# RWKV scan: key norms and group norms taken by a power of minus one half on GpSimd instead of a square root on ScalarE and a reciprocal on VectorE

## The reference, cut to what matters

```
kkf = split_heads(k * k_k)                       # 16 heads of 64 channels
kk  = kkf / maximum(sqrt(sum(kkf * kkf, -1)), 1e-12)      # the key norm, one number a token and head
...
mu  = y.mean over a head's 64 channels            # the group norm of the scan's output
var = square(y - mu).mean over the same 64
z   = (y - mu) * rsqrt(var + 64e-5) * lnx_g + lnx_b  + bonus, then times the gate
```

## Time and profile before

| | |
|---|---|
| time, median of 3 runs | 3846.18 us (3844.47 to 3848.1) |
| time of the profiled execution | 3840.48 us |
| its span in the profile | 3837.7 us |
| TensorE busy, share of the span | 92% |
| VectorE, GpSimd, ScalarE busy | 63%, 50%, 25% |
| mean granted TensorE clock | 0.967 of full speed |

### The profile page before, as it was taken

How to read it: one execution, slowest core, us unless ns; L and a number is a source line. 1 busy time by engine, 2 the same in 40 slices (tenths; PEclk the granted TensorE clock), 3 DMA queues, 4 the chain that set the end, 5 groups by cost and what they waited for, 6 DMA issues and landing times.

```text
span 3837.7 us, 74279 instructions
## 1 busy us (share of the span) xinstructions
PE 3525.7 (92%) x31772; PEld 3301.6 (86%) x31772; DVE 2402.6 (63%) x3149; ACT 962.6 (25%) x1950; POOL 1930.2 (50%) x1067
## 2 busy tenths in 40 slices
PE   7999999999789878889999994799999999999998
PEld 3877799999788678878999994799999777899997
DVE  5355688757784467746885768887586556622125
ACT  5333230001243355532300012300012333310010
POOL 1323456665365646626566561366564333466662
PEclk9899999999899899989999997899999999999999
DMA  8200134433145534332343331243332100122221
GB/s 322 64 12 17 41 103 138 137 115 117 69 142 180 152 85 103 83 95 66 113 146 120 124 102 41 78 148 128 115 125 69 36 18 18 56 77 77 73 77 50
DMA packets 226855, 367.66 MB, mean 96 GB/s; under 512 B 104752, under 2 KB 111088, under 8 KB 226416
## 3 DMA queue, kind: packets, MB, share of 16 engines
q1 hardware_dynamic: 171408, 255.08, 21.9%
q10 hardware_dynamic: 55136, 107.98, 8.1%
HBM read 326.47 MB, written 36.54 MB: 95 GB/s over the span
## 4 chain that ended last, share of the span: by engine, by line
PE 76%; DVE 12%; ACT 3%; issue 2%; DMA 2%; SPq 1%; POOL 1%; ACTq 0%; DVEq 0%; POOLq 0%
PE ps L851 58%; PE ps L1105 3%; PE ps L894 2%; PE ps L1118 2%; PE ps L1136 2%; DVE r_t L2544 1%; PE ps L911 1%; DVE x L2340 1%; DVE r_hlo L2528 1%; PE ps L1077 1%; PE ps L1059 1%; DVE ps L2693 1%; DVE x L2349 1%; DVE m_mx L2472 1%; DVE s_T L2692 1%
## 5 line engine op out<-in xcount | busy, mean ns | idle before, releaser
L678 POOL TENSOR_TENSOR w_hi<-w_raw,zrow 128x1024 fp32r<-128x1024 f32 x354 | 694.9, 1963 | 1246.6 <-PE ps L851 898.2
L680 POOL TENSOR_TENSOR w_lo<-w_raw,w_hi 128x1024 fp32r<-128x1024 f32 x354 | 900.6, 2544 | 27.8
L2242 DVE SCALAR_TENSOR_TENSOR f_acc<-f_unit,silu_c,f_acc 128x512 f32<-128x512 f32 x504 | 630.7, 1292 | 7.6
L851 PE MATMUL ps<-f_hhi,w_hi 128*128 128x320 f32 x2688 | 635.3, 318 | 0.0
L851 PE MATMUL ps<-f_hhi,w_lo 128*128 128x320 f32 x2688 | 613.7, 310 | 0.0
L851 PE MATMUL ps<-f_hlo,w_hi 128*128 128x320 f32 x2688 | 611.4, 309 | 0.0
L851 PEld LDWEIGHTS ps<-f_hlo,w_hi 128*128 128x128 f32 x2688 | 449.4, 188 | 0.0
L851 PEld LDWEIGHTS ps<-f_hhi,w_lo 128*128 128x128 f32 x2688 | 449.1, 188 | 0.0
L851 PEld LDWEIGHTS ps<-f_hhi,w_hi 128*128 128x128 f32 x2688 | 441.1, 189 | 0.0
L851 PE MATMUL ps<-f_ahi,w_hi 128*128 128x320 f32 x1408 | 322.7, 310 | 0.0
L851 PE MATMUL ps<-f_ahi,w_lo 128*128 128x320 f32 x1408 | 321.1, 309 | 0.0
(11 more groups left out here) (400 smaller groups left out, 6710.4 us busy)
## 6 DMA issues: line engine op xcount, KB each, us to landing
w_raw<-in_w SPq DMA_DIRECT2D x340, 512.0 KB, 3.6
f_unit<-in_ada_w ACTq DMA_DIRECT2D x72, 1024.0 KB, 6.2
ada_ring<-in_ada_w SPq DMA_DIRECT2D x24, 1024.0 KB, 6.5
up_scratch<-r_o ACTq DMA_DIRECT2D x40, 320.0 KB, 2.9
s_LW<-up_scratch SPq DMA_DIRECT2D x16, 320.0 KB, 4.9
s_LA<-up_scratch SPq DMA_DIRECT2D x8, 640.0 KB, 6.7
x<-in_x SPq DMA_DIRECT2D x1, 2560.0 KB, 9.6
x_scratch<-r_o ACTq DMA_DIRECT2D x8, 320.0 KB, 2.2
```

The lines of the kernel that those rows point to most:

```text
L678: nc.gpsimd.tensor_tensor(whi[:, slot, :], raw[:, raw_slot, :], zrow[:, 0:1].to_broadcast([P, CH * P]), ALU.add).then_inc(w_hi_done, 1)
L680: nc.gpsimd.tensor_tensor(wlo[:, slot, :], raw[:, raw_slot, :], whi[:, slot, :].bitcast(F32), ALU.subtract).then_inc(w_split, 1)
L851: last = mm(ps[:, 2 * b + h, 0:HT], w, r[:, h * HT:(h + 1) * HT], start=kt == 0 and n < 2, stop=kt == KT - 1 and n >= 4)
L2242: last = stt(acc[:, cd, :], unit[:, k, :], by, acc[:, cd, :], ALU.mult, ALU.add)
```

## The change

The square root on ScalarE and the reciprocal on VectorE go; a power of -0.5 on GpSimd comes in for both norms. For the key norm ScalarE only copies the sums out of PSUM, GpSimd clips them at 1e-24 (the sum, not its root) and takes the power between `centre` and `keys`; VectorE waits for that (`unit`) before it spreads. For the group norm GpSimd scales and adds the bias, then takes the power, inside `normed`. The last pair's group norm stays as it was.

```
 GpSimd
+                def unit_norms(j):
+                    pool.wait_ge(q.emptied, FILL["norm", j])
+                    ch(ts(m.nrm[:, :], m.nrm[:, :], 1e-24, None, ALU.max))
+                    tt(m.nrm[:, :], m.nrm[:, :], root.to_broadcast([P, 2 * NCH]), ALU.pow).then_inc(q.unit, 1)
...
                     tt(m.y2[:, :, :], m.v[j % 3][:, :, :], m.bon[j % 4][:, :].unsqueeze(2).to_broadcast(CC), ALU.mult)
-                    pool.wait_ge(q.trc, j + 1)
+                    ch(ts(m.var[:, :], m.var[:, :], 1.0 / 64, GN_EPS, ALU.mult, ALU.add))
+                    ch(tt(m.var[:, :], m.var[:, :], root.to_broadcast([P, NC]), ALU.pow))
...
                         total(i - 1)
                         centre(i - 1)
                     if 0 <= i + 3 < PAIRS:
+                        unit_norms(i + 3)
                         keys(i + 3)
 ScalarE
                     act.wait_ge(q.filled, FILL["norm", j])
-                    af(m.nrm[:, :], ps[:, 7, 0:2 * NCH], ACT.Sqrt, bias=eps[:, 3:4]).then_inc(q.emptied, 1)
+                    nc.scalar.copy(m.nrm[:, :], ps[:, 7, 0:2 * NCH]).then_inc(q.emptied, 1)
...
-                    if (s, n) == ((7, 1) if i < FINAL else (4, 1)) and 0 <= i - 1 < FINAL:
-                        deviation(i - 1)
 VectorE
                 def norms(j):
-                    dve.wait_ge(q.emptied, FILL["norm", j])
-                    ch(ts(m.nrm[:, :], m.nrm[:, :], 1e-12, None, ALU.max))
-                    ch(nc.vector.reciprocal(m.nrm[:, :], m.nrm[:, :]))
+                    dve.wait_ge(q.unit, j + 1)
                     cp(m.nkk[:, :].rearrange("p (a n) -> p a n", n=64), ...).then_inc(q.spr, 1)
...
-                def deviation(j):
-                    dve.wait_ge(q.rsd, j + 1)
-                    nc.vector.reciprocal(m.var[:, :], m.var[:, :]).then_inc(q.trc, 1)
...
-                        if 0 <= i - 1 < FINAL - 1:
-                            deviation(i - 1)
```

More of the change, by code:

```diff
@@ L242, in build @@
         cols = sb("ln_cols", [P, 8, NCH])
-        warm = cols[:, 7, 0:1]
+        warm, root = cols[:, 7, 0:1], eps[:, 4:5]
         sc_c = sb("silu_c", [P, KD, 2])
@@ L464, in build @@
         q_rwb = sems("rwb", "const ready ld ldr ldv ldg scan kys ex e0 ka kksq spr til prod filled emptied ast ald inv xst xld "
-                            "sc msk tk bk r rev u uev ds S0 S1 first y yev tsum tmu cen tsq tvar rsd trc zt zst sst vb st zlo back")
+                            "sc msk tk bk r rev u uev ds S0 S1 first y yev tsum tmu cen tsq tvar rsd unit zt zst sst vb st zlo back")
         s_zld = sem("rwb_zload")
@@ L699, in heads @@
                 ch = Chain(pool, chain_pool)
-                tt = nc.gpsimd.tensor_tensor
+                tt, ts = nc.gpsimd.tensor_tensor, nc.gpsimd.tensor_scalar
                 c3 = lambda t: t.rearrange("p (c t) -> p c t", c=NC)
@@ L2667, in final_norm @@
                     nc.vector.tensor_reduce(m.var[:, :], y2, AX.X, ALU.add).then_inc(q.tvar, 1)
-                    dve.wait_ge(q.rsd, j + 1)
+                    dve.wait_ge(q.rsd, 1)
                     ch(nc.vector.reciprocal(m.var[:, :], m.var[:, :]))
@@ L2769, in extras @@
                         lo_part(s - 5)
-                    if i == FINAL and s in (2, 4, 5):
-                        (mean, None, variance, deviation)[s - 2](FINAL - 1)
+                    if i == FINAL and s in (2, 4):
+                        (mean, None, variance)[s - 2](FINAL - 1)
                     if s <= 5 and ok(i + 1):
@@ L2866, in _ @@
             nc.vector.memset(eps[:, 2:3], GN_EPS)
-            nc.vector.memset(eps[:, 3:5], 0.0).then_inc(s_init, 1)
+            nc.vector.memset(eps[:, 3:4], 0.0)
+            nc.vector.memset(eps[:, 4:5], -0.5).then_inc(s_init, 1)
             dve.wait_ge(s_const, 32)
```

## The result

The changed kernel takes **3869.5 us** (median of 4 runs, 3868.58 to 3872.62), the kernel before 3845.3 us beside it (4 runs, 3841.06 to 3848.1): ratio 1.0066, 95% interval 1.0055 to 1.0078, so 24.2 us slower. The forecast was 3852 us and "same", with the same chance, 0.47, on "slower". The time lies inside the range (3843 to 3870), but at its upper end and on the side of the rivals. The profiled execution took 3872.62 us, with a span of 3870.7; it is 32.1 us above the one before (3840.48), 8 more than the medians differ, so a term read off the two traces may be some us too large.

What follows compares the result with a forecast made beforehand. TensorE was taken as the bound (busy 92%, 76% of the chain). Terms -5.1 + 0.6 - 0.4 + 5.6 + 4.7 + 0.4 = +5.8 us on 3840.48 gave 3846.3; with the median 5.7 above, 3852 us, range 3843 to 3870.

Steps and rivals of the forecast that it cites:

- the price x: Time of one 128 x 10 power on GpSimd, taken as 0.8 us, between 0.2 and 2.52.
- 1.5 + 5.5x: The forecast's whole sum in us as a function of the power's time; slower than noise from 1.13 us on.
- the power is dear: Rival, at VectorE's wait ahead of the spread: a power of 2.5 us gives 3861, of 4 us 3870; chance 0.36.
- the clock: Rival: TensorE's longer pause at the spread halves its clock in passes 1 to 4, 12 us more, 3864; chance 0.12.
- 4.7 + 0.4 - 0.4: Opening: spread in pass -2 behind splits +4.7 us, power in pass -3 +0.4, clip and reciprocal off VectorE in pass 0 -0.4.
- VectorE is busy without pause: Pass 0: with GpSimd idle the power is ready in time, so removing VectorE's clip and reciprocal gains 0.4 us.
- The loads' 5.1 us: ScalarE, passes 1 to 4: four table loads of 1.28 us on the chain go, a gain of 5.1 us.
- the power of the group norm is off the chain: GpSimd in `normed`: 1.2 us of added work cancels against 1.3 us of saved wait a pass, effect 0.
- the single load in pass -3: ScalarE: of 8 loads ahead of the exponentials (L1943) only the first one stays.
- the +0.6 of the tail: Last pair's group norm: the single square-root load moves there and costs 0 to 1.28 us, half taken.
- Absorbed: Rival: slack at corner V in passes 2 and 3 and value projections in pass -2 hide the delay, 3845; chance 0.12.
- every switch costs double: Rival: each ScalarE table load costs twice its row, so removal returns 10.3 us, sum +0.7, 3847; chance 0.03.

Runs made afterwards that it cites:

- e2: The changed kernel with both norms' powers replaced by a multiply by a constant; 7.3 us slower than the kernel before.
- e8: The changed kernel with only the key norms' power replaced by a multiply by zero; 9.9 us slower than the kernel before.
- e11: The changed kernel with the key norms' power issued twice; 37.4 us slower than the kernel before, 3879.3 us.
- e4: The changed kernel with GpSimd's clip and power of the key norm put ahead of `centre`; 7.8 us slower than the kernel before.
- e3: The changed kernel with 16 constant matmuls on TensorE ahead of its wait for the spread in passes 1 to 4; 19.3 us slower than the kernel before.
- e10: The changed kernel with the old key-norm path for the last four pairs, so the power serves only passes -3 to 0; 8.9 us slower than the kernel before.
- e1: The kernel before with the norms' square roots, except the last pair's group norm, made Identity, removing 15 table loads; 4.2 us faster than the kernel before.
- e6: The changed kernel with the old key-norm path in passes -3 to 0 and the power ahead of `centre`; 2.5 us slower than the kernel before.
- e12: The kernel with only group norms by power, plus a one-column exponential moving the table load into a ScalarE wait, passes 1 to 4; 0.2 us faster than before.
- e5: The changed kernel with the old key-norm path for the first four pairs (passes -3 to 0); 14.1 us slower than the kernel before.
- e9: The changed kernel with the old path for all key norms, so only group norms use the power; 1.5 us slower than the kernel before.

## Why the prediction was wrong

**The step that failed first is the price x.** "The nearest row is 0.40 us ... I take twice that, x = 0.8". It is 1.98, ten times the multiply of the same form (0.205, e2): the rows that the estimate was made from say nothing of a power. With 1.98 in the prediction's own formula, 1.5 + 5.5x, the sum is 12.4 instead of 5.8, and the rival "the power is dear" (from x = 1.13 on, slower) decides. Its mechanism is shown: the copy is 3.28 us later, e2, e8 and e11 move with x, e4 with its place. That the time still lies in the range is luck: the upper end was drawn for x = 4, while x = 1.98 alone gives about 3859, and the other 12 us come from terms that the sum didn't have.

**The second step is the clock, kept apart as a rival of 0.12.** It wasn't an alternative to the other cases but part of them all: with the power as cheap as a multiply (e2, e8) the pause is 2.7 us and the clock falls in every one of the four passes, so at the forecast's own x = 0.8 it would most likely have fallen too. The prediction's "against it", that passes 1 to 4 are denser than pass 0, did not hold. Its size was too high: 3 us in each pass was feared, and e3 shows 1.4 to 1.8 in the changed kernel, 5 to 6.5 in all. Some 3.5 to 4.6 of that came with the cheap multiply already; only the rest hangs on the price.

**The opening was undersized.** The forecast had 4.7 + 0.4 - 0.4, which is 6.5 with x = 1.98; e10 gives about 9. Two statements were wrong. "VectorE is busy without pause" in pass 0: in the trace before it idled there, 2.65 us up to the clip, and the copy follows at once,

```profile
1390.58 0.17 DVE L2601 TENSOR_SCALAR s_nrm<-s_nrm 128x10 f32<-128x10 f32 x1 [2.65 <-ACT s_nrm L1926]
```

so the power's time is in the open (copy 2.60 us behind ScalarE's, before 0.76). And in pass -3 the whole of x counts, not half: GpSimd's products wait for the keys that come behind the spread (1.32 us, before not at all), and the splits of pass -2 start 3.0 us later.

**The copy itself became slower,** which no step had. It took 0.49 us in passes -3 and 0 and 1.33 in passes 1 to 4; released by the power, it starts together with GpSimd's key products and takes 1.81. It is 0.49 when it starts ahead of GpSimd's next instruction (e4), which then takes 1.43 us instead of 1.26. The end of the 1.33 us copy is 0.35 us behind the end of `centre` in the trace before. This fits what the Trainium skill says (SBUF — State Buffer, "SBUF: two separate sides"): VectorE and GpSimd share a pair of ports, which an fp32 copy within SBUF uses too, and the one that starts first holds it for its whole instruction. In e3 the copy is as slow and V comes as early as it ever does (10.54 us), so in passes 1 to 4 it cost little. In the opening it is 1.3 us longer in passes -3 and 0 each (1.83 and 1.81), about what the opening lacks; in e2, where it takes 0.49 there, the opening is 151.8 us. No run separates it from the clock, which falls there too.

**The loads' 5.1 us** were right as a mechanism (1.63 us to 0.22 in the solve) and fit e1's median, but in the traces only part of it stays. From V to the end of the pass it is 8.64 us with the load and 7.23 without where nothing disturbs it; summed over four passes, e1, e4, e6 and e12 have 33.7 to 34.4 us against 34.9 before, not the 29.3 that four such gains give. Where the spread is late (the changed kernel, e2, e3, e5, e8, e11) it is 31.4 to 32.9, so 2 to 3.5 us are gained. In the first four kernels the half clock comes up in passes 1 to 4 for 6.8 to 27.2 us; before it is absent there, in e9, which keeps the loads, it begins only 2 us ahead of their end, but in e10, which keeps them too, it comes up for 13.6 us. So the clock is what most likely takes the rest of the gain, but no run shows it, nor that the closing of the gap brings the fall on.

The rest stood or was not tested: the power of the group norm is off the chain within e9's interval (0 to 8 us), the single load in pass -3 is there, and the +0.6 of the tail no run shows. "Absorbed" and "every switch costs double" fell: nothing was absorbed, e1 has no such gain.

The 24.2 us, put together: 5.8 as forecast, 6.5 for the price, 5 to 6.5 for the clock in passes 1 to 4, about 3 for the opening beyond the price; 2 to 4 are left. Loads that gave less than 5.1 can be in it, but the runs don't separate this.

## What to carry to other kernels

An operation that no row shows should not be priced by rows of another kind, and least of all taken near their lower end: where the verdict turns at 1.13 us, the forecast is that of the dear side until something shows otherwise. Moving a short step to an idle engine is free only if its place in that engine's queue is: behind an instruction that waits for the very engine to be relieved, a step of 2 us cost 14 us in four passes, and ahead of it nearly nothing. And where a wait ahead of TensorE grows, the lower clock behind it belongs into the same term, not among the rivals: here 2.7 us of wait were enough.

## What was not expected of the hardware

- A power of 128x10 elements on GpSimd takes 1.98 us, a multiply of the same form 0.205 us, a clip 0.25 us.
- After a pause of 4.45 us TensorE had half its clock for 6.8 us, in each of four passes; with 16 matmuls in the pause (3.84 us of them) and a wait of 0.68 us left it had all of it up to V, and the kernel's median was 5 us lower for doing more.
- After a pause of 2.65 to 2.78 us the clock fell as well, in all four passes of two kernels, for 3.4 us in seven of the eight; after the 0.67 us of the kernel before it stayed full.
- VectorE's copy of 128x640 takes 0.49, 1.33 or 1.81 us according to what GpSimd began before it.
